# Computing the neighbourhood mixer's values 256 columns at a time, in the two shared PSUM banks

## The reference, cut to what matters

```python
def neighbourhood_mixer(hx, hc, w_in, rpb, w_out, need_ctx_out):
    px = hx @ w_in                                  # 256 tokens x 4096
    q = px[..., :B_WIDTH]                           # B_WIDTH = 1024
    k = px[..., B_WIDTH:2 * B_WIDTH]
    v = px[..., 2 * B_WIDTH:3 * B_WIDTH]
    z = px[..., 3 * B_WIDTH:]
    pkv = hc @ w_in[:, B_WIDTH:3 * B_WIDTH]
    kc, vc = pkv[..., :B_WIDTH], pkv[..., B_WIDTH:]
    # per row of the grid: softmax over 8 x 16 neighbours with a bias, and all 256 context
    # tokens; then the weighted sum of v and vc
    yx = (o * jax.nn.silu(z)) @ w_out
```

## Time and profile before

| | us |
|---|---|
| median of 3 runs | 1441.73 |
| lowest, highest | 1441.57, 1443.01 |
| the profiled execution's own time | 1441.73 |
| its span, first to last instruction | 1439.8 |
| busy: PE, DVE, ACT, POOL | 1335.2, 890.8, 685.9, 339.2 |
| TensorE clock granted, mean over the span | 0.978 of full |

### The profile page before, as it was taken

The page is one execution under the profiler, slowest core; times in us unless marked ns, Lnnn a source line. Parts: engine busy times, 40 slices in busy tenths (PEclk is TensorE's granted clock), DMA queues, the critical chain, the costliest instruction groups (busy, mean ns, idle before and its releaser), DMA issues.

```text
span 1439.8 us, 24983 instructions
## 1 busy us (share of the span) xinstructions
PE 1335.2 (93%) x9224; PEld 1163.3 (81%) x9224; DVE 890.8 (62%) x1398; ACT 685.9 (48%) x1191; POOL 339.2 (24%) x373
## 2 busy tenths in 40 slices
PE   6979999999999998899999999899988897999777
PEld 4866799999998886798999998778844577889446
DVE  6858658777655887555777765445277437433764
ACT  5555345555444677444555544334276424224651
POOL 5921114333322040103333332102011211000011
PEclk9989999999999999999999999999999998999999
DMA  8564437666552542363666665132300362334100
GB/s 292 170 200 148 146 118 242 182 182 183 181 183 90 162 146 75 144 194 102 177 182 183 178 216 178 57 101 75 98 20 1 65 160 82 118 99 134 32 1 30
DMA packets 52368, 191.60 MB, mean 133 GB/s; under 512 B 6016, under 2 KB 6272, under 8 KB 51904
## 3 DMA queue, kind: packets, MB, share of 16 engines
q1 hardware_dynamic: 43344, 158.85, 36.2%
q0 software_dynamic: 8368, 31.33, 6.9%
q10 hardware_dynamic: 576, 0.31, 0.1%
HBM read 189.41 MB, written 1.05 MB: 132 GB/s over the span
## 4 chain that ended last, share of the span: by engine, by line
PE 73%; DVE 10%; issue 10%; ACT 4%; POOL 2%; DMA 1%; SPq 0%; DVEq 0%; POOLq 0%; ACTq 0%
PE G L392 13%; PE G L393 13%; PE G L394 13%; PE A L392 5%; PE A L394 5%; PE A L393 5%; PE R L557 3%; PE R L512 2%; DVE SM L1017 2%; PE G L868 2%; PE R L440 2%; ACT WH L1529 1%; DVE WL L951 1%; POOL RSQ L1987 1%; PE R L392 1%
## 5 line engine op out<-in xcount | busy, mean ns | idle before, releaser
L951 DVE TENSOR_TENSOR WL<-RAW,WH 128x1024 fp32r<-128x1024 f32 x295 | 384.1, 1307 | 371.8 <-ACT WH L1529 371.6
L1529 ACT ACTIVATE WH<-RAW 128x1024 fp32r<-128x1024 f32 x295 | 310.9, 1058 | 481.1 <-PE G L394 359.6
L392 PE MATMUL G<-XH,WH 128*128 128x256 f32 (+1 forms) x1408 | 424.2, 301 | 17.6 <-DVE XL L1310 7.5
L393 PE MATMUL G<-XL,WH 128*128 128x256 f32 (+1 forms) x1408 | 421.0, 299 | 0.0
L394 PE MATMUL G<-XH,WL 128*128 128x256 f32 (+1 forms) x1408 | 420.9, 299 | 0.0
L392 PEld LDWEIGHTS G<-XH,WH 128*128 128x128 f32 x1408 | 271.7, 193 | 29.0 <-issue 13.5
L393 PEld LDWEIGHTS G<-XL,WH 128*128 128x128 f32 x1408 | 271.8, 193 | 7.5
L394 PEld LDWEIGHTS G<-XH,WL 128*128 128x128 f32 x1408 | 271.7, 193 | 7.6
L392 PE MATMUL A<-HH,WH 128*128 128x256 f32 x352 | 99.8, 283 | 0.0
L393 PE MATMUL A<-HL,WH 128*128 128x256 f32 x352 | 99.6, 283 | 0.0
L394 PE MATMUL A<-HH,WL 128*128 128x256 f32 x352 | 99.6, 283 | 0.0
(11 more groups left out here) (316 smaller groups left out, 2251.6 us busy)
## 6 DMA issues: line engine op xcount, KB each, us to landing
RAW<-in_wst SPq DMA_DIRECT2D x295, 512.0 KB, 3.6
M<-in_wmod POOLq DMA_DIRECT2D x48, 512.0 KB, 5.8
B<-in_rpb POOLq DMA_DIRECT2D x4, 1024.0 KB, 11.7
H<-in_x_t SPq DMA_DIRECT2D x2, 512.0 KB, 9.1
M<-in_x_tok SPq DMA_DIRECT2D x1, 1024.0 KB, 12.9
M<-in_ctx_t POOLq DMA_DIRECT2D x1, 1024.0 KB, 5.1
out_y<-M SPq DMA_DIRECT2D x1, 1024.0 KB, 3.9
C<-in_cst SPq DMA_DIRECT2D x1, 737.0 KB, 14.6
```

Source lines behind the costliest of these rows:

```text
L392: mm(out, lh, rh, start=start, stop=False, skip_group_check=True)
L393: mm(out, lh, rl, start=False, stop=False, skip_group_check=True)
L951: v.tensor_tensor(WL[:, slot, :], RAW[:, raw, :], WH[:, slot, :].bitcast(F32), ALU.subtract).then_inc(w_lo, 1)
L1529: act(WH[:, slot, :], RAW[:, raw, :], ACT.Copy).then_inc(w_hi, 1)
```

## The change

`b_v` becomes eight units in `UNITS`. It has four groups instead of two; a group takes two panels and computes 256 output columns for all four token tiles. Two token tiles share a bank, so a group fills exactly `G[0]` and `G[1]`; the `A`, `R` and `O` banks are no longer used in this stage. The weights are laid out on the host for 256 columns a panel row instead of 512. ACT reads a group out with two copies, one for each bank, behind the second split of the group's `ahead(e)`.

```diff
@@ UNITS
-         ("b_q", 4), ("b_k", 8), ("b_z", 4), ("b_o", 4)]
+         ("b_q", 4), ("b_k", 8), ("b_v", 8), ("b_z", 4), ("b_o", 4)]
@@ PE
+            def value_unit(u, p, tts):
+
+                nb = len(tts) // 2
+                outs = [bank(u + b) for b in range(nb)]
+                for k in range(KD):
+                    if k % 4 == 0:
+                        take(p + k // 4)
+                    wh, wl = wtile((p + k // 4) % SPL, 2 * (k % 4), 2)
+                    for n, tt in enumerate(tts):
...
+                            at = 8 * (tt // 2) + k
+                            xh, xl = (x[:, at, (tt % 2) * P:(tt % 2 + 1) * P] for x in (XH, XL))
+                        m = mm3(outs[n // 2][:, (n % 2) * T:(n % 2 + 1) * T], xh, xl, wh, wl,
+                                k == 0 and n % 2 == 0, k == KD - 1)
+                    if k % 4 == 3:
+                        m.then_inc(w_used, 1)
...
-            value_unit(0)
-            evacuated(pe, U0["b_k"] + 6)
-            evacuated(pe, U0["b_k"] + 7)
-            value_unit(1)
-            pe.wait_ge(tm_v, TVALS + 10)
+            for g in range(4):
+                value_unit(U0["b_v"] + 2 * g, START["b_v"] + 2 * g, (0, 1, 2, 3))
...
-            pe.wait_ge(tm_v, TVALS + 12)
             attention("b", scores_b, value_b)
@@ DVE
-            for g in range(2):
-                ahead(START["b_v"] + 4 * g + 4)
+            for g in range(4):
+                ahead(START["b_v"] + 2 * g + 2)
@@ ACT
-            for g in range(2):
-                e = START["b_v"] + 4 * g + 4
-                ahead(e - 1)
-                for tt in range(4):
-                    if tt < 3:
-                        ac.wait_ge(tm_mm, len(FIRST) + len(TOKEN) + 9 + 3 * g + tt + 1)
-                    else:
-                        ac.wait_ge(w_used, e)
-                    act(V2[:, tt, g * 512:(g + 1) * 512], sets[g][tt], ACT.Copy).then_inc(tm_v, 1)
+            for g in range(4):
+                e = START["b_v"] + 2 * g + 2
                 ahead(e)
+                ac.wait_ge(w_used, e)
+                for b in range(2):
+                    u = U0["b_v"] + 2 * g + b
+                    act(V2[:, 2 * b:2 * b + 2, g * T:(g + 1) * T], G[u % 2][:, :].rearrange("p (a c) -> p a c", a=2),
+                        ACT.Copy).then_inc(bank_free[u % 2], 1)
@@ host
-"b_v": _value_tiles(w_b[:, 2048:3072], 4),
+"b_v": _value_tiles(w_b[:, 2048:3072], 2),
```

More of the change, by code:

```diff
@@ L431, in gemm_unit @@
                         i += 1
+            def value_unit(u, p, tts):
[6 more added lines that the diff above has]
+                    for n, tt in enumerate(tts):
+                        if nb == 1:
+                            xh, xl = XH[:, k, tt * P:(tt + 1) * P], XL[:, k, tt * P:(tt + 1) * P]
+                        else:
+                            at = 8 * (tt // 2) + k
[4 more added lines that the diff above has]
+                        m.then_inc(w_used, 1)
             def row_stats(name, out=R):
@@ L1950, in _ @@
                 ahead(START["b_k"] + u + 1)
-            for g in range(2):
-                e = START["b_v"] + 4 * g + 4
-                ahead(e - 1)
-                for tt in range(4):
-                    if tt < 3:
-                        ac.wait_ge(tm_mm, len(FIRST) + len(TOKEN) + 9 + 3 * g + tt + 1)
-                    else:
-                        ac.wait_ge(w_used, e)
-                    act(V2[:, tt, g * 512:(g + 1) * 512], sets[g][tt], ACT.Copy).then_inc(tm_v, 1)
-                ahead(e)
+            for g in range(4):
+                e = START["b_v"] + 2 * g + 2
+                ahead(e)
+                ac.wait_ge(w_used, e)
[3 more added lines that the diff above has]
+                        ACT.Copy).then_inc(bank_free[u % 2], 1)
             for u in range(4):
@@ L2211 @@
         "a_z": _tiles(w_a[:, 1536:][:, perm]), "a_o": _tiles(a["a_w_out_2"][0][perm]),
-        "b_q": _tiles(w_b[:, :1024]), "b_k": _tiles(w_b[:, 1024:2048]), "b_v": _value_tiles(w_b[:, 2048:3072], 4),
+        "b_q": _tiles(w_b[:, :1024]), "b_k": _tiles(w_b[:, 1024:2048]), "b_v": _value_tiles(w_b[:, 2048:3072], 2),
         "b_z": _tiles(w_b[:, 3072:]), "b_o": _tiles(a["b_w_out_2"][0]),
```

## The result

| | us |
|---|---|
| before, median of 4 runs (1440.38 to 1443.01) | 1441.65 |
| after, median of 4 runs (1458.71 to 1460.84) | 1459.74 |
| ratio over all executions, with its 95% interval | 1.0121 [1.0108, 1.0134] |
| predicted | 1460.2 (1456 to 1465), +18.5 |
| the profiled execution after, and its span | 1457.8, 1456.0 |

The changed kernel takes 1.0121 times as long, 17.4 us (15.6 to 19.3) more on 1441.65. The ratio rests on 11 executions of the changed kernel, whose median is 1458.90; the two medians of 4 in the table lie 18.1 us apart. The profiled execution after is one of the faster ones; its span is 16.2 us longer than that of before.

A forecast was written before the change was run, and what follows sets the result against it. PE was taken to bound the kernel, with no idle time in `b_v`. 2.54 + 3.43 + 7.50 + 2.00 = 15.5 us, plus 3.0 for two clock falls, makes 18.5 on 1441.73: 1460.2 us, range 1456 to 1465.

The forecast's parts named there:

- What bounds the stage: In `b_v`, PE is busy 43.50 of 43.50 us at full clock; anything that makes PE wait goes into the time.
- Part 1: Matmuls of `b_v`: 384 of 256 columns instead of 192 of 512 cost +2.54 us, bounds 0 to 5.
- Part 2: From `b_k` to `b_v`: the first matmul waits for DVE's read-out of the last `b_k` unit, 3.43 us.
- refill: Behind a gap, PE's first matmul is followed by the next after 0.31 us instead of 0.23, 0.08 more.
- Part 3: Three edges between groups inside `b_v`: PE waits for ACT's split and both copies, 2.50 us each, 7.50 in all.
- Part 4: From `b_v` to `b_z`: the first unit waits for the split and the read-out of G0 alone, 2.00 us.
- What goes: The waits on `tm_v` ahead of `b_z` and the attention go; they cost nothing, so nothing is given back.
- Part 5: Five new gaps in PE's stream may lower the clock: two falls taken, +3.0 us, between 0 and 7.5.
- the rival without falls: Waits in and around `b_v` as priced, but no fall of the clock: 1457.2 us, chance 0.13.
- both theories: For edges behind `b_v` groups without the split: one clock fall less, 1454.4 us, or falls independent of gap length, 1455.9.
- the rival's value: For lengthened edges behind `b_v` groups: equally many clock falls at either gap length, 1463.8 us, or +22.1; no chance given.

The follow-up runs named there:

- the width alone: The changed kernel, but each group of two panels in `b_v` has two banks of its own; ratio 1.0023 to the kernel before, +3.3 us.
- shorter gaps: The changed kernel with ACT's two copies ahead of the split that the same matmul releases; ratio 1.0094 to the kernel before, +13.5 us.
- longer ones: The changed kernel with two needless ACT copies of 128x512 ahead of each group's real ones; ratio 1.0171 to the kernel before, +24.6 us.

## Why the prediction was right

- **What bounds the stage.** Right: the earlier trace rows showed PE full, and every wait added went into the time.
- **Part 1, the width.** +2.54 forecast, +2.55 measured with the width alone.
- **Part 2, the entry.** 3.43 forecast; measured 1271.21 - 1267.87 = 3.34, and 0.08 of refill, 3.42. The chain was running hidden in the trace before, so its length could be read there.
- **Part 3, the inner edges.** 2.50 forecast; the last matmul of a group starts at 1298.14, the next was due at 1298.26 and came at 1300.64, so 2.38, with the refill 2.46. Three are 7.4. The chain was shown by moving its parts: with the split behind the copies an edge is 1.0 us shorter, and with the two banks filled one after the other the whole edge is gone.
- **Part 4, ahead of `b_z`.** 2.00 forecast, 1.85 and the refill measured, 1.93.
- **What goes.** Nothing was given back by the removed waits, as forecast: the attention of before and after begins at the same distance behind `b_z`, 24.9 and 25.0 us behind its first matmul.
- **Part 5, the clock.** Two falls forecast; 2, 2 and 1 in three profiles, at (13.08 - 0.08 - 11.51) = 1.49 us each, where 1.5 was forecast. By the times it is less: 17.4 less 15.3 for the measured width and waits leaves 2.1 us, 1.4 falls, which is where most of the 1.1 us between forecast and result lies. The number came out right, but the weights within it were wrong, so that it did is in part luck: I counted the inner gaps nearly like the entry's. The entry's gap brought a fall in 6 of 6 profiles, an inner one of 2.22 us in 2 of 9.

One reading under part 5 was also wrong. I took it from the earlier trace rows that the clock stayed full behind the gap of 1.90 us at the end of `b_z`, and the rival without falls had this as its only support. But PE was busy for only 1.99 of the 4.6 us of that row, since a second wait of 2.67 us lies in it, and the next stretch of the same profile is at the low level:

```profile
1341.50:1344.90 3.40, 3.34 (x10) 1.84 (x11) 2.52 (x6) 1.46 (x5) 0.00 (x0) 0.50 0.00 0
```

Whether the first gap, the second or both brought that fall is open. The row was no evidence for gaps that bring no fall; the table's seven gaps of 0.7 to 1.7 us are.

Sum in the profile: 46.04 for the matmuls, 3.42, 7.39, 1.85 and 2.98 for two falls is 61.68 us, the stage to a hundredth. Between the spans there are only 16.2 of its 18.2 us. The rest lies outside the change: this execution reached `b_v` 0.6 us earlier, and it has no fall of the clock at the end of the last attention, where the profile of before had one (clock 0.76 in 1392 to 1399, 1.6 us). Falls elsewhere in the program come and go too, each worth about as much as the one in question, which is why single profiles are compared by stage here.

The Trainium skill's advice against idle gaps above about 3 us (TensorE: Matmul & The Clock Gate, Why this matters for your kernels) fits these counts better than I had allowed: 8 of the table's 10 falls are behind gaps of over 3 us. But a fall came behind 2.22 us twice. What is shown of the clock is a count of falls against gap lengths, in few profiles; why one gap of 2.22 us brings a fall and the next doesn't stays open. That the time of a whole run follows the number of falls is only weakly shown: with shorter gaps the interval holds both theories, and with longer ones the rival's value lies only 0.5 us outside it.

## What to carry to other kernels

Where two banks are filled and read out in turn, a group must not keep both open to its end: finish one bank, then the other, and read the first out meanwhile, and the read-out hides; the same work cost 2 us in that order and 17 in the other. Behind the last matmul of a stage, look at what stands in the reading engine's list ahead of the read-out and is released by the same matmul. When a wait is shortened, follow the next one on each engine: here the microsecond came back twice, first on DVE, then on POOL, before it could be kept.

## What the runs showed of the hardware

A POOL cast of 128x256 took 0.40 us alone and 1.32 us beside a DVE subtraction of two SBUF operands of 128x1024 (1.22 us), and it ended 0.25 us behind that (1403.94 against 1403.69). In the kernel before, all 24 casts of this kind took 0.40 us. The kernels with the split behind and inside the attention have two of 1.32 us each, and each of the four began 0.15 us behind such a subtraction. The Trainium skill (GPSIMD Engine Reference, Key points) says that GpSimd shares its SBUF interfaces with VectorE and contends with its instructions of two SBUF inputs; the trace agrees, with 0.92 us here.

The pace of 256-column matmuls in the fast format at full clock was the same to a thousandth of a us, 0.120, with the weights as the stationary operand (`b_z`) and with the activations (`b_v` in the changed kernel).
